# Identity products on TensorE ahead of five waits in a two-block kernel (first norm, second norm, last weighing)

## The reference, cut to what matters

```python
def first_block(x, ...):
    h = rms_norm(x, norm1_g)                  # the first norm
    z = h @ w_in                              # 28 tiles of 128 columns
    ... y_mix from a gated recurrence and a short convolution ...
    x = x + y_mix @ w_out
    u = causal_dwconv(rms_norm(x, norm2_g) @ w_up, ffn_conv_w)
    gate, up = split(u)
    x = x + (gelu(gate) * up) @ w_down        # the stream called DOWN
    return rms_norm(x, final_g)               # called the second norm below

def second_block(x, ...):
    h = x @ w_in_2
    ... latent attention: 4 heads, 8 blocks of 128 queries, v weighed by the softmax ...
    return layer_norm(alpha * x + mix, ln_g, ln_b)
```

## Time and profile before

| | |
|---|---|
| time of three runs | 1727.75, 1729.96, 1732.75 us; median 1729.96 |
| profiled execution, first to last instruction | 1726.5 us (the page gives this span and no other time of that execution) |
| mean granted TensorE clock | 0.992 |
| TensorE matmul busy | 1681.0 us, 97% of the span |
| VectorE, ScalarE, GpSimd busy | 71%, 46%, 30% |
| share of TensorE in the chain that ended last | 82% |

### The profile page before, as it was taken

How to read it: one execution, slowest core, us unless ns; L and a number is a source line. 1 busy time by engine, 2 the same in 40 slices (tenths; PEclk the granted TensorE clock), 3 DMA queues, 4 the chain that set the end, 5 groups by cost and what they waited for, 6 DMA issues and landing times.

```text
span 1726.5 us, 20915 instructions
## 1 busy us (share of the span) xinstructions
PE 1681.0 (97%) x7556; PEld 1383.3 (80%) x7556; DVE 1225.3 (71%) x1442; ACT 792.4 (46%) x1038; POOL 516.6 (30%) x284
## 2 busy tenths in 40 slices
PE   7999999999999999999999999998999999999998
PEld 6888878888877888888888888886878877777776
DVE  6577772259999888888888789885636365666554
ACT  5466541235764434343434455553322146676531
POOL 4221222200015555554552000003432242345320
PEclk8999999999999999999999999999999999999999
DMA  8111112152422232222223876651321320110251
GB/s 259 49 36 49 40 45 74 37 201 80 152 81 76 83 97 73 84 84 87 73 86 125 317 237 199 219 159 43 122 74 61 85 86 25 37 49 25 102 215 73
DMA packets 161095, 176.96 MB, mean 102 GB/s; under 512 B 13566, under 2 KB 114692, under 8 KB 161028
## 3 DMA queue, kind: packets, MB, share of 16 engines
q1 hardware_dynamic: 158724, 167.67, 30.3%
q10 hardware_dynamic: 2304, 8.39, 1.3%
HBM read 140.38 MB, written 35.65 MB: 102 GB/s over the span
## 4 chain that ended last, share of the span: by engine, by line
PE 82%; DVE 10%; ACT 4%; issue 1%; POOL 1%; DMA 1%; POOLq 0%; DVEq 0%; ACTq 0%; SPq 0%
PE ps L921 28%; PE ps L2398 24%; PE ps L2352 18%; PE ps L2618 4%; PE ps L2603 3%; PE ps L2648 2%; PE ps L2588 1%; DVE lat L2109 1%; PE ps L2576 1%; DVE pt_lo L2203 1%; DVE prob L2185 1%; POOL z_lo L1015 1%; PE ps L2279 1%; DVE square_dve L1636 0%; ACT pt_hi L1548 0%
## 5 line engine op out<-in xcount | busy, mean ns | idle before, releaser
L945 POOL TENSOR_TENSOR w_lo<-w_raw,w_hi 128x1024 fp32r<-128x1024 f32 x52 | 135.8, 2614 | 623.0 <-ACT w_hi L1044 623.0
L2398 PE MATMUL ps<-hop_hi_P,wop_hi_P 128*128 128x512 f32 x672 | 262.5, 391 | 4.7 <-DVE u L1853 3.3
L2398 PE MATMUL ps<-hop_hi_P,wop_lo_P 128*128 128x512 f32 x672 | 261.5, 389 | 0.0
L2398 PE MATMUL ps<-hop_lo_P,wop_hi_P 128*128 128x512 f32 x672 | 261.5, 389 | 0.0
L921 PE MATMUL ps<-h_hi,w_hi 128*128 128x512 f32 x752 | 235.1, 394 | 11.3 <-DVE h_lo L1621 7.8
L951 POOL TENSOR_TENSOR wop_lo_P<-pair_sum,wop_hi_P 128x512 fp32r<-128x512 f32 x90 | 135.9, 1510 | 354.5 <-ACT wop_hi_P L1055 354.5
L921 PE MATMUL ps<-h_lo,w_hi 128*128 128x512 f32 x752 | 232.9, 391 | 0.0
L921 PE MATMUL ps<-h_hi,w_lo 128*128 128x512 f32 x752 | 232.7, 391 | 0.0
L921 PEld LDWEIGHTS ps<-h_hi,w_hi 128*128 128x128 f32 x752 | 141.4, 189 | 43.3 <-issue 14.0
L921 PEld LDWEIGHTS ps<-h_lo,w_hi 128*128 128x128 f32 x752 | 142.1, 189 | 29.8
L921 PEld LDWEIGHTS ps<-h_hi,w_lo 128*128 128x128 f32 x752 | 142.0, 189 | 29.7
(11 more groups left out here) (350 smaller groups left out, 3337.9 us busy)
## 6 DMA issues: line engine op xcount, KB each, us to landing
pair_raw<-in_w_up SPq DMA_DIRECT2D x48, 512.0 KB, 4.6
w_raw<-in_w_in SPq DMA_DIRECT2D x46, 512.0 KB, 3.9
dn_raw<-gu_park SPq DMA_DIRECT2D x84, 256.0 KB, 3.9
dn_raw<-in_w_down SPq DMA_DIRECT2D x60, 256.0 KB, 3.1
gu_park<-up_cv SPq DMA_DIRECT2D x24, 512.0 KB, 2.6
out_raw<-in_w_out SPq DMA_DIRECT2D x30, 256.0 KB, 3.0
x_tok<-in_x SPq DMA_DIRECT2D x4, 1024.0 KB, 8.2
x_park<-xs SPq DMA_DIRECT2D x1, 4096.0 KB, 14.3
```

What stands on the lines that cost most here:

```text
L945: nc.gpsimd.tensor_tensor(lo[:, :], raw[:, :], hi[:, :].bitcast(f32), ALU.subtract).then_inc(w_lo_done, 1)
L2398: mm = nc.tensor.matmul(dst, w[q][:, k, :], x[q][:, k, :], start=a, stop=b, skip_group_check=True)
```

## The change

It adds a helper that multiplies the identity by itself a given number of times, each product into 128 columns of a PSUM tile that nothing reads, and calls it in five places on TensorE's program. Each of the products opens and closes its own accumulation. Two of the places also get a wait. Nothing is taken out, and no other engine's program changes.

```diff
+            def keep_busy(dst, count):
+                for _ in range(count):
+                    nc.tensor.matmul(dst, ident[:, :], ident[:, :], start=True, stop=True)
 ...
             for t in range(NT):                      # the 64 transposes of x_tok
 ...
                 mm.then_inc(xt_done, 1)
+            keep_busy(ps[3][:, HALF:HALF + P], 20)
             pe.wait_ge(rows_in, 16 * 16)
             pe.wait_ge(setup_done, POS_F)
 ...
             spread(ps[2]).then_inc(rb_done, 1)
 ...
+            keep_busy(ps[3][:, HALF:HALF + P], 32)
             pe.wait_ge(xt_copied, NT)
             first_two(0, (ps[0], ps[1]), 0)
 ...
             for p in range(4):
                 last_steps(DOWN, p)
+            pe.wait_ge(product_added, DOWN.added(10))
+            keep_busy(ps[2][:, HALF:HALF + P], 18)
             pe.wait_ge(x1_squares, squared(DOWN, 16))
             mean_squares(scr[4], ps[2]).then_inc(ms_done, 1)
             pe.wait_ge(rstd_done, 3)
             spread(ps[3]).then_inc(rb_done, 1)
 ...
+            keep_busy(ps[2][:, HALF:HALF + P], 32)
             first_two(N_IN2, (ps[0], ps[1]), 1)
 ...
                     if i >= 2:
                         pe.wait_ge(ya_done, i - 1)
+                    if i == 2 * HEADS - 1:
+                        pe.wait_ge(ya_done, i)
+                        keep_busy(ps[3][:, 0:P], 16)
                     weigh(i)
```

## The result

The changed kernel takes 1736.60 us in the median of five executions (1734.28 to 1737.14); the kernel before, timed beside it, 1729.67 (1727.48 to 1732.75). The ratio is 1.0035, interval 1.0021 to 1.0049: slower by 0.35%, about 6 us (the two medians lie 6.9 apart), where +1.6 was forecast. The median is 0.1 us above the top of the range given, 1736.5; the ratio put on the 1729.96 that the forecast started from gives 1736.0, just inside it. "Slower by over 0.3%" had been given 6 in 100.

What follows compares the result with a forecast made beforehand. TensorE, busy 97% of the span, was taken to bound the kernel, with low clock after its waits as the possible gain. 0.3 + 1.5 - 0.2 = +1.6 us on 1729.96 gave 1731.6, range 1726.5 to 1736.5.

Steps and rivals of the forecast that it cites:

- Price of a product: All five calls: a float32 product is two matmul records, 0.222 us warm and 0.427 cold.
- Rivals 2 and 3: All calls: a product costs one record, -6.3 us, chance 0.06; or products don't hold the clock, +26 us, chance 0.05.
- Rival 4: First norm: transposes don't count for the clock, half of 3.3 to 4.9 us lost, in all +3.6, chance 0.04.
- the rule that the prediction weighed there: First norm's first products, after transposes: full clock doesn't engage for transpose-mode work, so they would run cold.
- Rival 2's sum: First norm -3.0, second -1.7, last weighing -1.65, in all -6.3 us, 1723.6, chance 0.06.
- Place 1: First norm, 20 products before the row transposes: VectorE 0.4 us earlier; ScalarE and GpSimd about 1.3 us later, but hidden.
- third low part: First norm, needed by k = 3: ready at 32.6 us or a little earlier, no bound.
- Places 1 and 2: First norm, 20 and 32 products: clock gives back 2.4 us, overrun takes 2.7; k = 3 at 33.6, +0.3 us.
- I put the same on the median shown: Whole kernel: the +1.6 us worked out on the 1726.5 us span, put on the 1729.96 median, gives 1731.6.
- Places 3 and 4: Second norm, 18 and 32 products: spread's end unchanged, then k = 3 at 1193.0 instead of 1191.53, +1.5 us.
- Rival 1: Second norm: clock falls around `mean_squares` all the same, +1.7, in all +3.3 us, 1733.3, chance 0.21.
- Place 5: Before the last weighing, 16 products: `weigh(7)` starts later but runs warm, ending at 1635.5 against 1635.7, -0.2 us.

Runs made afterwards that it cites:

- half counts: The change with 10, 16, 9, 16 and 8 products instead of 20, 32, 18, 32 and 16: 1729.11 us, ratio 0.999 to the kernel before.
- Place 1 alone: Kernel before plus only the 20 products ahead of the first norm's row transposes: 1732.11 us, ratio 1.0011.
- The full counts of places 3 to 5 alone: Kernel before plus only the 18 and 32 products of the second norm and the 16 before the last weighing: 1733.61 us, ratio 1.0016.
- second profile of the change: The changed kernel timed and profiled once more, no edit: 1735.19 us, ratio 1.0029 to the kernel before.
- fourth profile of before: The kernel before, no edit, in the last of its repeat profiles: 1729.60 us.
- place 2 alone: Kernel before plus only the 32 products between the first norm's spread and `first_two`: 1729.79 us, ratio 0.9996.

## Why the prediction was right or wrong

**Price of a product, "I take 0.222".** Right: 3.57 us for 16, records 0.111 apart. Rivals 2 and 3 fell with it. Rival 4 did too: the products of place 1 started warm, behind nothing but transposes, so the rule that the prediction weighed there does not hold in these rows. Rival 2's sum was also wrong in itself: half counts, which take just the times that it supposes, gave -0.6 us and not -6.3.

**Place 1, "0.4 us earlier for VectorE", the delay of ScalarE and GpSimd "hidden".** Here a step failed, though k = 3 came within 0.15 us. VectorE did start 0.35 us earlier (24.97 against 25.32), but the delay was not hidden. What I called the third low part is that of tile 3, GpSimd's second. I took it to be ready at 32.6; it was ready at 33.69, since the weights' low parts ended at 26.6, and VectorE's first low part beside them took 2.74 us and GpSimd's first 3.38:

```profile
26.58 3.38 POOL L958 TENSOR_TENSOR h_lo<-scr,h_hi 128x1024 fp32r<-128x1024 f32 x1
```

In the profile of before the two took 1.34 and 2.39. So the row wait does stand on the path, through ScalarE, GpSimd and `h_lo`. That the instant still fitted is luck: TensorE's own overrun happened to be as long (its last pair of matmuls before k = 3 started at 33.12, at 0.45 us a pair). Place 1 alone shows the path without it.

**Places 1 and 2, "+0.3".** Right against the profiled execution (+0.41). But the kernel before usually gets to k = 3 earlier: the four profiles have 33.3, 31.6, 32.8 and 32.3, mean 32.5, and the three profiles with both full calls 33.7, 33.5 and 34.0, mean 33.75. So the size against the median is +1.2. This is the term that was mis-sized in the sum that I put on the median: my "I put the same on the median shown" took the late k = 3 of one execution for the rule.

**Places 3 and 4, "+1.5".** Right: +1.54 and +1.57 in the two profiles of the change. Rival 1 (the clock falls around `mean_squares` all the same) did not come in these, but it came in the profiles of all four other kernels that have place 3. The full counts of places 3 to 5 alone took 21.5 us to k = 3, +3.2 against before, which is rival 1's price of 3.3. Of the kernels with nine products there none kept the clock. So rival 1 is real; how often it comes with 18 products is not told by three profiles.

**Place 5, "-0.2".** Right, -0.21. With eight products instead of 16 it is -1.6 to -1.7, in all three kernels that had them.

**What was missing: the two stretches without a product.** +3.90 and +2.95 us in the first profile of the change, nearly all by low clock near 494, 1231 and 1412. Three of four profiles of the unchanged kernel have the falls near 484 and 494, and the second profile of the change lacks those near 1231 and 1412. So the 8.3 us between the two first profiles is not the size of the change: about 3 of the 3.90 us are there because the first profile of before lacked its usual falls. That the range held, or nearly, is luck as well: the forecast and rivals 1 and 4 ended at 1733.6, and only the allowance for the spread of the runs above that covers a cost whose larger part no term of the sum had.

**Small misreadings.** By the prediction's own working, give 31.8 and 1629.2 for two changes of the clock that it has at 31.7 and 1629.4. Only rival 4's "4.9" rests on one of them; it would be 5.0.

**What stays open.** Against the fourth profile of before, whose time is that of the median, the change's stretches differ by +1.4, +1.0, +1.6, +2.9 and -0.2 us. Stretches one, three and five explain 2.8 of the 6 us measured (1.0029 and 1.0035, intervals down to 1.0015, 2.6 us). The rest is mostly low clock elsewhere. In the second profile of the change the five differences are +1.2, +1.3, +1.6, -0.2 and -0.2 us.

The executions that were only timed have their mean clock on record. Of the twelve of the change, nine had 0.994 or 0.995 and took 1734.28 to 1737.14 us; the profile with the three falls is one of them. The other three, the profile without the falls near 1231 and 1412 among them, had 0.996 or 0.997 and took 1731.94, 1733.31 and 1734.94 us. So most executions of the change have more low clock than its second profile; where it lies in them is not on record. The fastest, at 0.997, is 2.8 us above the 1729.14 of the kernel before beside it, which is about what stretches one, three and five give. (Between kernels the mean clock doesn't rank the times: the change has 0.994 against 0.992 and is slower, for part of the low clock of before fell into waits.)

None of the four profiles of before has a fall between its second norm and the last weighing; of the ten profiles of other kernels five have (a stretch of 436 us or more). And the kernels that have products in the first norm and the old code in the second took 19.7 to 21.0 us to k = 3 there, the four of before 18.2 to 18.4. That points to a real effect of the change on the clock in stretches behind it, but one profile per kernel is too little to show it. Its cause was not tested and stays open.

## What to carry to other kernels

Filling TensorE's wait gives back only what TensorE's low clock costs, and only as far as no other engine is late at the same point: VectorE's and GpSimd's low parts kept most of it in the first norm. An overrun is paid wherever TensorE is what the next stage waits for, and an overrun ahead of an operation that another engine's program waits for can be paid on that path too, as place 1 shows; place 2 alone overran by 1 us and paid nothing. Whether a shorter call holds the clock must be looked at place by place: eight products did so ahead of the last weighing in three profiles of three, nine ahead of `mean_squares` in none of three.

Count the records of a product in the trace (two for float32 by float32) before choosing a number. And where executions of one kernel differ in where the clock is low, take several profiles of the kernel before: one execution's late or cold stretch is no baseline for what warming it would give.

## What the runs showed of the hardware that was not expected

VectorE's subtraction of two float32 tiles (line 1621) takes 1.23 us alone and 2.7 to 3.4 us beside GpSimd's line 945, in each of the ten profiles in which the spread was early or warm; in the four others, with less of line 945 beside it, it took 1.34 to 1.83. GpSimd's own (line 958) takes 2.4 us, and 3.4 the first time in the same ten. It took away two thirds of what an early spread gives at the start of the projection: in the kernel before the projection began at 25.7 us after a spread that ended at 19.7, and at 26.8 after one that ended at 22.8. The Trainium skill, page "Advanced Engine Details and Errata", section "GPSIMD Details", says that GpSimd shares a read and a write interface with VectorE and conflicts with its instructions that have two SBUF inputs; the rows agree (1.23 against 2.7 to 3.4 us).

The clock fell within 4 us of the start of the sixteen one-column matmuls (line 2272) in twelve of fourteen profiles; only the two of the change kept it. Two stretches of one-column matmuls near 481 and 491 to 494 (line 2411) stand where one or two falls are seen in twelve of the fourteen too: in the third and fourth profile of before the mean clock is 0.84 over 480 to 501, although matmuls cover all 21 us there. And the kernel before, on one chip, went from 1727.3 to 1734.6 us along with its mean clock: of 35 executions, those with 0.992 or 0.993 lay at 1727.3 to 1730.4, those with 0.988 or 0.989 at 1733.3 to 1734.6.
